# Odd attention of a two-layer decoder step: both units of a pair turned ahead of the next scores, a sample step's scores ahead of its key transposes

## The chip, the cores and the metric

The kernel runs on one core of a Trainium2 chip. The time is device microseconds (us) of one execution; lower is better. TensorE (PE) multiplies and transposes, VectorE (DVE), ScalarE (ACT) and GpSimd (POOL) work element by element, SyncE (SP) starts most DMAs. The engines run their own instruction streams in program order and meet at semaphores.

## The reference

Two layers of a hybrid decoder are run for a prompt (512 tokens, width 1024) and for 8 samples of one token each with a cache of 256 positions. Layer 0 mixes with a gated convolution and a matrix memory, layer 1 with two attentions; an MLP with squared relu follows each. The change is in layer 1, in this part:

```python
def odd_attend(...):                       # per block of 128 queries; f32
    ...
    # compressed: softmax over 64-token blocks, o_c
    # selected (8 blocks at most, "s"), sliding window of 256 ("w"), and top-k keys of the indexer ("d"):
    s_w = jnp.einsum('btgrd,blgd->btgrl', qn, kw[:, :, 0]).astype(f32) * scale - m_n[:, :, None] * dist_w[...]
    p_w = masked_softmax(s_w, mask_w[:, None, None, :])
    o_w = jnp.einsum('btgrl,blgd->btgrd', p_w.astype(kw.dtype), kw[:, :, 1])
    o_n = gates[..., 0:1] * o_c + gates[..., 1:2] * o_s + gates[..., 2:3] * o_w
    ...
    o_d = jnp.einsum('btgrk,btkgd->btgrd', p_d.astype(sel_d.dtype), sel_d[:, :, :, 1]).reshape(bn, tq, -1)
```

The samples' attention is the same over their cached keys and one new key. Every branch has 8 heads in 2 groups.

## The kernel before, in words

All weights stream through a ring in SBUF; the projections and the MLPs are long runs of matmuls 128x128 by 260 (line 1024), with each operand split into a high and a low part. Between the odd layer's input projection and its output projection lies the attention stage.

The prompt's attention is cut into 96 **units**: one block of 128 queries (i), one head (p of 4, g of 2) and one branch ("d", "s" or "w"). A unit has 1 to 4 key blocks of 128. Units u and u+1 with u even are a **pair**: the same queries, branch and p, for g = 0 and 1. The first 32 units are of branch d, the next 32 of s and w for query blocks 2 and 0, the last 32 of s and w for blocks 1 and 3. For one unit the work goes round the engines:

- `pair_scores` (line 1488): PE forms the scores of both units of a pair, in banks 0 and 1. It waits for `q_sc`, VectorE's reduction of the pair before.
- line 2694: VectorE adds the position table and finds the row's extreme, then counts `q_sc`.
- line 1909: ScalarE forms the exponential and its sum (ACTIVATE and a read of the accumulator), then counts `q_e`.
- `unit_turned` (line 1503): PE transposes the unit's 1 to 4 blocks into bank 2 (u even) or 3 (u odd). It waits for `q_e` of the unit and for `q_te`, u-1, which says that unit u-2 has been copied out of that bank.
- line 1920 (traced as line 1599, the helper): ScalarE copies the turned unit to SBUF and counts `q_te`.
- `pair_values` (line 1518): PE multiplies with the values, into bank 5 or 6; it waits for `q_te` of both units.
- `end_of` (line 1533): after the last unit of a job (one query block and branch), PE spreads the inverse sums, or adds the compressed branch, in bank 2.

The order is written out by a loop over steps t = 0 to 99 on each engine. In PE's loop (line 1561) step t has `unit_turned(t - 3)`; an odd step has also `pair_scores(t + 1)` and `pair_values(t - 5)`, and ends fall in odd steps. VectorE in step t reduces unit t. ScalarE in step t (line 1902) forms the exponential of unit t, then copies unit t - 3, then does sample work; from step 70 it also converts a weight tile in every third step. So ScalarE copies unit t - 4 right after the exponential of unit t - 1.

Sample work is laid between the units: in PE's even steps t = 12 + 2k runs `sample_step(k)` (line 1378), in the odd ones after them `sample_rest(k)`. Four times, from k = 0, 10, 19 and 28 on, `cached_keys(st, ...)` (line 1353) runs for st = 0 to 4: it transposes cached keys of two samples into bank 4 (st 0 to 3) and forms the scores of the two samples turned in the step before (st 1 to 4). ScalarE copies the turned keys into one of two buffers, `kTs`, and counts `bt_ev`. Both parts of `cached_keys` wait for the same value of it. Transposes are traced as line 982, all other matmuls of the stage as line 986; a transpose is 128x128, scores use 64 rows (64*128), values 64 columns (128*64), sample matmuls 32 or 64 columns.

Of the kernel before, what the change touches and what calls it, by code (L numbers as in the profile page):

```python
# [49 lines left out]
LS = PAST + 1  # L50
# [27 lines left out]
def build(nc, x_prompt, x_sample, state_conv, state_C, state_n, state_m, cache_kv, cache_idx, cache_win, page_table,  # L78
# [20 lines left out]
    with ExitStack() as ctx:  # L99
# [3 lines left out]
        def sem(name):  # L103
            return ctx.enter_context(nc.semaphore(name))
# [30 lines left out]
        ps = [ctx.enter_context(nc.psum_tensor(f"ps{i}", [P, 512], F32)) for i in range(8)]  # L135
# [21 lines left out]
        sm = {n: sem(n) for n in names}  # L157
# [378 lines left out]
        kTs = [room[:, 2 * LS * i:2 * LS * (i + 1)].rearrange("p (b k) -> p b k", b=2) for i in range(2)]  # L536
# [70 lines left out]
        units = []  # L607
# [371 lines left out]
        def _(pe):  # L979
            def tr(out, in_, n):  # L980

                return pe.matmul(out, in_, ident[0:n, 0:n], start=True, stop=True, is_transpose=True,  # L982
                                 skip_group_check=True)

            def mm(out, lhsT, rhs, start=True, stop=True):
                return pe.matmul(out, lhsT, rhs, start=start, stop=stop, skip_group_check=True)  # L986
# [166 lines left out]
            for k in range(KD):  # L1153
                last = tr(ps[7][:, B * k:B * k + B], xs_stage[:, P * k:P * k + P], B)
# [35 lines left out]
            for idx in range(len(E_TILE)):  # L1190
                if idx:
                    split_tile(G_IN0 + idx, xh1, hl)
                if idx == 5:
                    pe.wait_ge(sm["wc_in"], 16 * 8)
                    for s in range(2):
                        last = tr(ps[7][:, BLK * s:BLK * (s + 1)], wcK[0:64, P * s:P * s + P], 64)
                    last.then_inc(sm["tin"], 1)
                if idx == 2:
# [4 lines left out]
                    for half in range(2):  # L1203
                        last = mm(ps[4 + half][0:4, 0:H2], ident[0:8, 4:8], gz[:, half * H2:(half + 1) * H2])
                    last.then_inc(sm["fg_mm"], 1)
                if idx == 12:
# [7 lines left out]
                    for i in range(4):  # L1214
                        last = tr(ps[7][:, 16 * i:16 * i + 16], scs[:, P * i:P * i + P], 2 * B)
# [4 lines left out]
                if idx in (16, 18, 20, 22):  # L1220
# [6 lines left out]
                    for n, t0 in ((4, 12), (6, 16)):  # L1227
                        for b in range(B):
                            last = tr(ps[n + b // 4][:, P * (b % 4):P * (b % 4) + P],
                                      big[:, t0 + h, S + b:S + b + 1].to_broadcast([P, P]), P)  # L1230
                    last.then_inc(sm["head_mm"], 1)
                if idx == 25:
# [3 lines left out]
                    for i in range(4):  # L1236
                        last = tr(ps[5][0:B + 2, P * i:P * i + P], big[:, i, S - 2:T], P)
# [9 lines left out]
            for h in range(MH):  # L1247
# [6 lines left out]
                for n, t0 in ((2, 20), (3, 16)):  # L1254
                    for i in range(QT):
                        last = tr(ps[n][:, P * i:P * i + P], big[:, t0 + h, P * i:P * i + P], P)
# [3 lines left out]
                for i in range(QT + 1):  # L1260
# [5 lines left out]
                    if i >= 1:  # L1266
                        j = i - 1
                        pe.wait_ge(sm["p_ok"], QT * h + j + 1)
                        if j == 0:
# [8 lines left out]
                           stop=(j == QT - 1)).then_inc(sm["pv_mm"], 1)  # L1278
# [3 lines left out]
                for j in range(QT):  # L1282
                    last = mm(ps[4][:, 0:P], vw[:, P * j:P * j + P], ktm[:, P * j:P * j + P], start=(j == 0),
                              stop=(j == QT - 1))
                last.then_inc(sm["cn_mm"], 1)
                for j in range(QT):
                    last = mm(ps[5][0:1, 0:P], wsc[:, j:j + 1], ktm[:, P * j:P * j + P], start=(j == 0),
                              stop=(j == QT - 1))
# [21 lines left out]
            for idx, name in enumerate(O_NAMES):  # L1310
# [6 lines left out]
                if 4 <= idx <= 6:  # L1317
# [7 lines left out]
                    for c0 in range(0, i + 1, 2):  # L1325
                        c1 = min(c0 + 2, i + 1)
                        for e in range(4):
                            if n and not c0:
                                pe.wait_ge(sm["isc_r"], 4 * (n - 1) + e + 1)
                            r = slice(32 * e, 32 * e + 32)  # L1330
                            last = mm(ps[4 + e][:, P * c0:P * c1], big[r, L["qi"], P * i:P * i + P], kiz[r, P * c0:P * c1])
# [14 lines left out]
            for s, name in enumerate(SLOTS):  # L1346
                if s >= 4:
                    pe.wait_ge(sm["tm_a"], s - 3)
                for i in range(QT):
                    last = tr(ps[4 + s % 4][:, P * i:P * i + P], big[:, L[name], P * i:P * i + P], P)  # L1350
                last.then_inc(sm["tm_mm"], 1)

            def cached_keys(st, n0, lhs_of, src_of, key_rows, acc_rows):


                if 0 <= st < 4:
                    if n0 + st:
                        pe.wait_ge(sm["bt_ev"], n0 + st)
                    else:
                        pe.wait_ge(sm["pct_ev"], 1)  # L1360
                    for b in range(2):
                        for t in range(2):
                            last = tr(ps[4][0:key_rows, 256 * b + P * t:256 * b + P * t + P], src_of(2 * (st + 4 * b) + t), P)
                    last.then_inc(sm["bt_mm"], 1)
                if 1 <= st <= 4:
                    pe.wait_ge(sm["bt_ev"], n0 + st)
                    for b in range(2):
                        bb = st - 1 + 4 * b
                        r = 32 * b if acc_rows == 64 else 0
                        last = mm(ps[7][r:r + 32, 0:LS], lhs_of(bb)[:, r:r + 32], kTs[(st - 1) % 2][0:key_rows, b, :],  # L1370
                                  start=(st == 1 and r == 32 * b), stop=(st == 4 and (b == 1 or acc_rows == 64)))
                    last.then_inc(sm["bs_mm"], 1)

            def new_col(j, col):

# [91 lines left out]
            def compressed_step(t):  # L1467

                if 1 <= t <= QT:
                    pe.wait_ge(sm["kc_ok"], 1)  # L1470
                    i = t - 1
                    for p in range(NP):
                        last = mm(ps[7][:, 64 * i + 16 * p:64 * i + 16 * p + 16], big[:, L[f"qn{p}"], P * i:P * i + P], KCZ)
                    last.then_inc(sm["pc_mm"], 1)
                if t == QT:
                    for p in range(NP):
                        last = tr(ps[4][0:64, P * p:P * p + P], VF[:, p, :], P)
                    last.then_inc(sm["vf_mm"], 1)
                if t == 10:
                    pe.wait_ge(sm["vf_ev"], 1)  # L1480
                    pe.wait_ge(sm["pc_n"], 1)
                    for i in range(QT):
                        last = tr(ps[4][0:64, P * i:P * i + P], sc[:, 64 * i:64 * i + 64], P)
                    last.then_inc(sm["pct_mm"], 1)
# [3 lines left out]
            def pair_scores(u):  # L1488

                i, p, _, br, k0, o = units[u]  # L1490
                q = L[f"q{'d' if br == 'd' else 'n'}{p}"]
                ends_at = sorted({min(i + 1, k0 + 2), i + 1})
                for c0, c1 in zip([k0] + ends_at, ends_at):
                    for g in range(2):
                        if u >= 2 and c0 == k0:
                            pe.wait_ge(sm["q_sc"], u + g - 1)
                        r = slice(HD * g, HD * g + HD)
                        last = mm(ps[g][:, P * (c0 - k0):P * (c1 - k0)], big[r, q, P * i:P * i + P],
                                  big[r, L["k" + br], P * c0:P * c1])
                        if c1 == i + 1:  # L1500
                            last.then_inc(sm["q_mm"], 1)

            def unit_turned(u):
                i, p, g, br, k0, o = units[u]
                pe.wait_ge(sm["q_e"], u + 1)
                if u >= 2:
                    pe.wait_ge(sm["q_te"], u - 1)
                if u + 1 in ends:
                    kind, x = ends[u + 1]
                    if kind == "sums":  # L1510
                        pe.wait_ge(sm["q_r"], x + 1)
                    else:
                        pe.wait_ge(sm["q_g"], end_no[kind, x] + 1)
                for b in range(i + 1 - k0):
                    last = tr(ps[2 + u % 2][:, P * b:P * b + P], Pb[u % 6][:, P * b:P * b + P], P)
                last.then_inc(sm["q_t"], 1)

            def pair_values(u):

                i, p, _, br, k0, o = units[u]  # L1520
                if u == first_of[o] and o >= 2:
                    pe.wait_ge(sm["q_g"], end_no["sums", o - 2] + 1)
                pe.wait_ge(sm["q_te"], u + 2)
                for b in range(i + 1 - k0):
                    for g in range(2):
                        r = slice(HD * g, HD * g + HD)
                        v = tm[:, k0 + b, P * VS[br] + HD * g:P * VS[br] + HD * g + HD]
                        last = mm(acc(o)[r, P * p:P * p + P], v, PTb[(u + g) % 4][:, P * b:P * b + P],
                                  start=(p == 0 and b == 0), stop=(b == i - k0))
                        if b == i - k0:  # L1530
                            last.then_inc(sm["q_o"], 1)
# [24 lines left out]
            for s, name in enumerate(SLOTS):  # L1556
                last = tr(ps[2 + s // 4][0:B, P * (s % 4):P * (s % 4) + P], big[:, L[name], S:T], P)
# [3 lines left out]
            for t in range(len(units) + 4):  # L1561
                if t == 3:
                    pe.wait_ge(sm["tms_ev"], 2)
                if 0 <= t - 3 < len(units):
                    unit_turned(t - 3)
                if t % 2 and t + 1 < len(units):
                    pair_scores(t + 1)
                if t % 2 and t >= 5:
                    pair_values(t - 5)
                if t in ends:  # L1570
                    end_of(t)
                compressed_step(t)
                if t >= START:
                    if (t - START) % EVERY == 0:
                        sample_step((t - START) // EVERY)
                    if (t - START) % EVERY == 1:
                        sample_rest((t - START) // EVERY)
# [1161 lines left out]
```

## Time and profile before

| | us |
|---|---|
| median of 3 runs | 1422.44 (1422.29 to 1427.97) |
| profiled execution, first to last instruction | 1421.2 |
| PE busy | 1366.7 |
| VectorE busy | 745.3 |
| ScalarE busy | 504.6 |
| attention stage | 807 to 981 |

The profile gives the span of one execution, from its first to its last instruction; for what lies around the span it has no figure of its own. "Busy" counts the time in which an engine has an instruction under way; starts of PE's matmuls are exact and their ends are modelled, so the distance from start to start tells what one costs. "Idle before" is time in which the engine had nothing under way, with the instruction that ended it.

### The profile page before, as it was taken

The page shows a single profiled execution, that of the slowest core. Times are in us where ns is not written, and L with a number is a line of the kernel's source. Part 1 is how long each engine was busy: PE and PEld are TensorE (multiplying, and loading weights), DVE is VectorE, ACT ScalarE, POOL GpSimd, SP SyncE. Part 2 cuts the span into 40 slices and gives each one's busy share as a digit, 9 for nine tenths or more (in the row PEclk, how much of TensorE's full clock was granted, in tenths as well). Part 3 has the DMA queues.
Part 4 walks back from the last instruction along what each step waited for, and adds up shares of the span by engine and source line. Part 5 has one row for each costly group of instructions (what it writes and reads, how often), then busy time and mean ns, then how long its engine had stood idle before and what let it go on. Part 6 is the DMA issues. An engine that isn't in the chain of part 4 may idle for free. (4 is left out here: it accounts for less than half of the span.)

```text
span 1421.2 us, 27641 instructions
## 1 busy us (share of the span) xinstructions
PE 1366.7 (96%) x11359; PEld 1287.3 (91%) x11359; DVE 745.3 (52%) x1378; ACT 504.6 (36%) x1004; POOL 397.1 (28%) x470
## 2 busy tenths in 40 slices
PE   6999998999999999999899999999999999999996
PEld 5999975899999999999899966667999999999996
DVE  3424777667434343343879856454774343343435
ACT  3321224345314023032542366786553032140311
POOL 3014423365101010014744473023652010010102
PEclk9999999999999999999999999999999999999998
DMA  5343170030323131312323226204113313132301
GB/s 156 125 114 107 43 238 6 3 119 31 126 83 117 63 119 60 119 60 52 60 90 60 64 82 216 61 2 120 64 56 120 119 60 119 60 119 69 110 31 60
DMA packets 87196, 123.86 MB, mean 87 GB/s; under 512 B 24438, under 2 KB 42302, under 8 KB 87040
## 3 DMA queue, kind: packets, MB, share of 16 engines
q1 hardware_dynamic: 82048, 107.00, 23.6%
q0 software_dynamic: 5024, 15.10, 3.6%
q8 instruction: 91, 1.49, 0.4%
q14 instruction: 33, 0.27, 0.1%
HBM read 115.62 MB, written 8.57 MB: 87 GB/s over the span
## 5 line engine op out<-in xcount | busy, mean ns | idle before, releaser
L1024 PE MATMUL ps<-xh,ring_lo 128*128 128x260 f32 (+2 forms) x2496 | 503.5, 283 | 1.4 <-ACT big L1599 1.4
L1024 PEld LDWEIGHTS ps<-xh,ring_lo 128*128 128x128 f32 (+2 forms) x2496 | 382.6, 187 | 3.3 <-ACT big L1599 2.3
L1024 PE MATMUL ps<-xl,wr 128*128 128x260 f32 x1568 | 351.4, 283 | 6.1 <-DVE xl L2070 3.9
L1024 PE MATMUL ps<-xh,wr 128*128 128x260 f32 x1568 | 352.9, 284 | 2.5 <-POOL xl L824 1.2
L1024 PEld LDWEIGHTS ps<-xl,wr 128*128 128x128 f32 x1568 | 255.2, 188 | 8.2 <-DVE xl L2070 5.1
L1024 PEld LDWEIGHTS ps<-xh,wr 128*128 128x128 f32 x1568 | 256.0, 188 | 5.0 <-ACT att L1636 1.4
L842 POOL TENSOR_TENSOR att<-att 128x520 f32<-128x520 f32 (+1 forms) x80 | 77.3, 967 | 548.6 <-DVE att L1996 521.5
L1972 DVE TENSOR_TENSOR ring_lo<-ring,wr 128x1024 fp32r<-128x1024 f32 (+1 forms) x144 | 192.1, 1337 | 62.1 <-ACT wr L1599 62.0
L1024 PE MATMUL ps<-hh,wr 128*128 128x260 f32 x1024 | 222.1, 283 | 0.0
L1024 PE MATMUL ps<-hh,ring_lo 128*128 128x260 f32 x1024 | 221.8, 283 | 0.0
L1024 PE MATMUL ps<-hl,wr 128*128 128x260 f32 x1024 | 221.7, 283 | 0.0
L1599 ACT ACTIVATE wr<-ring 128x1024 fp32r<-128x1024 f32 (+1 forms) x162 | 167.4, 1049 | 130.1 <-PE ps L1024 120.4
L1024 PEld LDWEIGHTS ps<-hh,wr 128*128 128x128 f32 x1024 | 164.5, 188 | 0.2 <-issue 0.2
L1024 PEld LDWEIGHTS ps<-hh,ring_lo 128*128 128x128 f32 x1024 | 164.5, 188 | 0.0
L1024 PEld LDWEIGHTS ps<-hl,wr 128*128 128x128 f32 x1024 | 164.0, 188 | 0.0
L1636 ACT ACTIVATE att<-ps 128x260 f32<-128x260 f32 x64 | 24.6, 384 | 304.4 <-PE ps L1024 304.4
L1983 DVE TENSOR_TENSOR xT<-xT,ps 128x260 f32<-128x260 f32 x96 | 37.5, 422 | 162.9 <-PE ps L1024 162.9
L1996 DVE TENSOR_SCALAR att<-ps 128x260 f32<-128x260 f32 x64 | 27.4, 428 | 137.4 <-PE ps L1024 137.4
L1024 PE MATMUL ps<-hl,ring_lo 128*128 128x260 f32 (+1 forms) x464 | 93.4, 283 | 0.0
L1599 ACT ACTIVATE big<-ps 128x260 f32<-128x260 f32 (+6 forms) x104 | 40.3, 402 | 148.5 <-PE ps L1024 133.2
L789 POOL TENSOR_TENSOR ring_lo<-ring,wr 128x1024 fp32r<-128x1024 f32 x18 | 43.3, 2412 | 109.8 <-ACT wr L1599 109.8
L986 PE MATMUL ps<-big 128*64 128x128 f32 (+3 forms) x504 | 66.7, 348 | 4.8 <-DVE small L2694 3.3
(354 smaller groups left out, 1620.8 us busy)
## 6 DMA issues: line engine op xcount, KB each, us to landing
ring<-in_w_up SPq DMA_DIRECT2D x16, 2048.0 KB, 7.9
ring<-in_w_down SPq DMA_DIRECT2D x16, 2048.0 KB, 7.9
ring<-in_w_in_e SPq DMA_DIRECT2D x9, 1024.0 KB, 5.6
ring<-in_w_in_e SPq DMA_DIRECT2D x2, 2048.0 KB, 8.8
ring<-in_w_out_e SPq DMA_DIRECT2D x2, 2048.0 KB, 8.8
ring<-in_w_in_o SPq DMA_DIRECT2D x16, 256.0 KB, 5.0
ring<-in_cache_kv POOLq DMA_DIRECT2D x32, 128.0 KB, 2.4
ring<-in_w_out_o SPq DMA_DIRECT2D x8, 512.0 KB, 8.9
```

Source lines behind the costliest of these rows:

```text
L789: pool.tensor_tensor(w_l, w_raw(u), w_h.bitcast(F32), ALU.subtract).then_inc(sm["w_lo_p"], 1)
L842: pool.tensor_tensor(hid[j % 2][:, cc], rel[j % 2][:, cc], rel[j % 2][:, cc], ALU.mult).then_inc(sm["hid_sq"], 1)
L986: return pe.matmul(out, lhsT, rhs, start=start, stop=stop, skip_group_check=True)
L1024: last = pe.matmul(bank(g, half)[0:width(g), 0:H2], w[:, k, :], x[:, k, cols(half)], start=first, stop=final)
L1599: return act.activation(out, in_, ACT.Copy, scale=scale)
L1636: act.activation(rel[j % 2][:, 0:H2], psA(g)[:, 0:H2], ACT.Relu).then_inc(sm["free_a"], 1)
L1972: dve.tensor_tensor(w_l, w_raw(u), w_h.bitcast(F32), ALU.subtract).then_inc(sm["w_lo"], 1)
L1983: last = (dve.tensor_tensor(x, x, y, ALU.add) if scale is None else dve.scalar_tensor_tensor(x, x, scale, y, ALU.mult, ALU.add))
L1996: dve.tensor_scalar(rel[j % 2][:, H2:T], psB(g)[:, 0:H2], 0.0, None, ALU.max).then_inc(sm["free_b"], 1)
```

## The change

In PE's loop an odd step t now turns unit t - 3 and unit t - 2, one behind the other, ahead of `pair_scores(t + 1)`; an even step turns nothing. In `cached_keys` the scores of the samples turned in the step before are formed first, and the next key transposes come behind them. Waits, banks and counts stay as they were, and no other engine's stream is touched.

```diff
@@ -1353,6 +1353,14 @@ def cached_keys(st, n0, lhs_of, src_of, key_rows, acc_rows):
+                if 1 <= st <= 4:
+                    pe.wait_ge(sm["bt_ev"], n0 + st)
+                    for b in range(2):
+                        bb = st - 1 + 4 * b
+                        r = 32 * b if acc_rows == 64 else 0
+                        last = mm(ps[7][r:r + 32, 0:LS], lhs_of(bb)[:, r:r + 32], kTs[(st - 1) % 2][0:key_rows, b, :],
+                                  start=(st == 1 and r == 32 * b), stop=(st == 4 and (b == 1 or acc_rows == 64)))
+                    last.then_inc(sm["bs_mm"], 1)
                 if 0 <= st < 4:
                     if n0 + st:
                         pe.wait_ge(sm["bt_ev"], n0 + st)
@@ -1362,14 +1370,6 @@
                     last.then_inc(sm["bt_mm"], 1)
-                if 1 <= st <= 4:
-                    ...                                  (the eight lines above)
@@ -1561,8 +1561,9 @@
             for t in range(len(units) + 4):
                 if t == 3:
                     pe.wait_ge(sm["tms_ev"], 2)
-                if 0 <= t - 3 < len(units):
+                if t % 2 and 0 <= t - 3 < len(units):
                     unit_turned(t - 3)
+                    unit_turned(t - 2)
                 if t % 2 and t + 1 < len(units):
                     pair_scores(t + 1)
                 if t % 2 and t >= 5:
```

## Rows read from the trace of the kernel before

**Rows 1.** The page: span, and engines' busy time, share of span, instructions.
```profile
span 1421.2 us, 27641 instructions
PE 1366.7 (96%) x11359; PEld 1287.3 (91%) x11359; DVE 745.3 (52%) x1378; ACT 504.6 (36%) x1004; POOL 397.1 (28%) x470
```
**Rows 2.** Busy time by stretch: stretch, length, engines, granted PE clock, DMA, GB/s.
```profile
821.06:835.30 14.24, 11.90 (x79) 8.43 (x79) 8.26 (x29) 6.55 (x20) 10.41 (x17) 0.76 0.05 8
835.30:980.95 145.65, 139.41 (x1404) 96.18 (x1402) 79.05 (x297) 102.97 (x315) 40.88 (x53) 1.00 0.36 101
```
**Rows 3.** PE's waits in 807 to 981: total us, times, longest.
```profile
PE ps L986 <- DVE small L2694: 3.3, 4, 1.9
PE ps L986 <- ACT att L1599: 1.8, 5, 0.8
PE ps L986 <- ACT big L1599: 1.7, 3, 0.8
PE ps L986 <- DVE ring L2590: 0.7, 1, 0.7
```
**Rows 4.** Timeline of PE around 883: start, us, instruction, count, idle before.
```profile
882.30 0.33 PE L982 MATMUL ps<-ident,big 128*128 128x128 f32 x1
882.56 0.49 PE L986 MATMUL ps<-big 64*128 64x128 f32 x4
...
883.78 0.33 PE L982 MATMUL ps<-ident,big 128*128 128x128 f32 x1
883.95 0.60 PE L982 MATMUL ps<-ident,ring 128*128 128x128 f32 x4
884.48 0.63 PE L986 MATMUL ps<-ring,small 128*32 128x257 f32 x4
```
**Rows 5.** Timeline of all engines in step 45.
```profile
890.80 0.56 DVE L2694 CUSTOM_DVE_ANT_0 att<-small,ps 128x384 f32<-128x384 f32 x1 [1.58 <-PE ps L986]
...
891.40 0.61 ACT L1909 ACTIVATE att<-att,small 128x384 f32<-128x384 f32 x1 [0.25 <-DVE small L2694]
...
891.65 0.72 PE L986 MATMUL ps<-big 64*128 64x128 f32 x4
...
891.92 0.19 ACT L1909 ACTIVATION_READ_ACCUMULATOR att<-att,small 128x1 f32 x1
...
892.01 0.47 ACT L1599 ACTIVATE att<-ps 128x384 f32<-128x384 f32 x1
...
892.53 0.88 PE L986 MATMUL ps<-att,big 128*64 128x128 f32 x12 [0.15 <-ACT att L1599]
```
**Rows 6.** Timeline in steps 13, 29 and 93: exponential and scores.
```profile
835.98 0.72 ACT L1909 ACTIVATE att<-att,small 128x512 f32<-128x512 f32 x1 [1.64 <-DVE small L2694]
...
836.65 0.49 PE L986 MATMUL ps<-big 64*128 64x128 f32 x4
...
867.35 0.61 ACT L1909 ACTIVATE big<-big,small 128x384 f32<-128x384 f32 x1 [1.60 <-DVE small L2694]
...
867.37 1.17 PE L986 MATMUL ps<-big 64*128 64x256 f32 x4 [0.28 <-DVE small L2694]
...
969.54 0.61 ACT L1909 ACTIVATE att<-att,small 128x384 f32<-128x384 f32 x1
...
970.28 0.70 PE L986 MATMUL ps<-big 64*128 64x256 f32 x4
```
**Rows 7.** Timeline of ScalarE in step 81.
```profile
949.37 1.05 ACT L1599 ACTIVATE wr<-ring 128x1024 fp32r<-128x1024 f32 x1
...
950.32 0.50 ACT L1909 ACTIVATE att<-att,small 128x256 f32<-128x256 f32 x1
```
**Rows 8.** Timeline of PE in step 9.
```profile
828.42 0.80 PE L986 MATMUL ps<-big 64*128 64x128 f32 x2 [1.89 <-DVE small L2694]
```
**Rows 9.** Timeline of PE at the end of the stage.
```profile
975.00 1.09 PE L986 MATMUL ps<-ident,small 128*64 128x128 f32 x16 [0.84 <-ACT att L1599]
...
976.89 0.52 PE L982 MATMUL ps<-ident,big 128*128 128x128 f32 x3 [0.31 <-ACT big L1599]
...
979.27 0.88 PE L986 MATMUL ps<-big 128*64 128x128 f32 x12 [0.58 <-ACT big L1599]
```

More of the change, by code:

```diff
@@ L1364, in cached_keys @@
                     last.then_inc(sm["bt_mm"], 1)
-                if 1 <= st <= 4:
[L1366 to L1372, printed above, removed]
             def new_col(j, col):
```

## The prediction

> **What bounds the kernel now.** I read the page first: TensorE (PE) is busy for 96% of the span, no other engine above 52% [rows 1]. So a change counts by the PE time that it takes out and by the PE idle time that it makes or closes. Then the stretches: the diff touches PE's order in the odd attention only, from 807 to 981 us. Past 835.3 us PE is busy 139.4 of 145.7 us at a granted clock of 1.00. In the 14 us before, it is busy 11.9 and the clock averages 0.76 [rows 2]. Third, PE's waits there: 3.3 us on the score reduction of VectorE, 3.5 us on ScalarE's copies, 0.7 us on the sample index scores [rows 3]. PE does one thing after another there, nearly gap-free, and everything after the stage starts when it ends. So what PE loses here reaches the end of the kernel one to one; nothing behind it (PE-bound multiplications) gives it back.
>
> Last, the order in time of single units, on which the prediction rests. I write T(u), S(u), V(u) for the turning (transposes), scores and values of unit u; R, E, C for VectorE's reduction, ScalarE's exponential and ScalarE's copy of the turned unit. Before, odd step t runs T(t-3), S of units t+1 and t+2, V of t-5 and t-4; even step t+1 runs T(t-2) and the sample work. After, odd step t runs T(t-3), T(t-2), S, V, and the even step only sample work.
>
> **Part 1: fewer changes of matmul shape (a gain).** A transpose inside a block of transposes costs 0.11 us. One alone between matmuls of other shapes takes 0.26 us to the next start (882.30 to 882.56); the one at 883.78 is first of a block and takes 0.17, and the four after it take 0.53, so the last one takes 0.20 [rows 4]. A block therefore costs 0.06 at its first and 0.09 at its last transpose on top: 0.15 us per block. Before, an even step with sample matmuls in it reads V | T | sample matmuls | T | S: two blocks. After, V | sample matmuls | T T | S: one. For steps that turn sample keys as well this needs the second edit, which puts the score matmuls first so that the key transposes join the next block. From the code such steps are: k = 1 to 7 and 9, 11 to 14, 18, 20 to 23, 27, 29 to 32, 36, and step 4 with the compressed scores: 24, less the two (k = 20, 29) where sample transposes precede anyway. 22 x 0.15 = 3.3 us off. Steps without sample matmuls keep one block: nothing. Bounds: 0 to 24 x 0.15 = 3.6.
>
> Here the Trainium skill would argue otherwise. "TensorE: Matmul & The Clock Gate", Part 3, under what overlaps and what doesn't, says that a weight load overlaps matmuls in flight only when the row groups differ. Transposes use all rows, so by that a transpose next to a transpose would overlap as little as one next to a matmul, and merging blocks would save nothing. This trace doesn't agree: 0.11 us inside a block against 0.17 and 0.20 at its ends.
>
> **Part 2: the wait that the second transpose brings forward (a loss).** T(t-2) writes the bank that unit t-4 used, so it waits for C(t-4) (semaphore q_te). ScalarE works in program order: C(t-4) stands behind E(t-1), which needs R(t-1), which needs S(t-1), and S(t-1) was issued one odd step earlier. Before, the same C(t-4) was awaited by V in step t, behind S(t+1), and by T(t-2) after that. Now T(t-2) stands ahead of S(t+1), so the chain S, R, E, C, T, S closes once per pair of units. Behind the waiting transpose stand S, V, the end and sample work; R and E of the next pair wait for that S.
>
> Worked out for step 45 [rows 5]: R(44) starts 890.80, E(44) runs 891.40 to 892.11 with its accumulator read, C(41) 892.01 to 892.48, and V starts 892.53 after a wait of 0.15. T(43) can't start before 892.53 either. PE would be free for it at 891.65 (start of S(46)) less 0.09 (no change of shape there) less 0.33 (the three transposes of unit 41, done a step earlier): 891.24. Idle: 1.29 us. The chain from score end (890.77) to T is 1.76 us; PE has only V(38,39) and T(42) to fill it.
>
> The same subtraction for each odd step (end of the exponential, plus the copy's end 0.18, 0.28, 0.38 or 0.49 us behind it for 1, 2, 3 or 4 blocks, plus 0.05, less PE's free time) gives a positive wait in: step 13 1.21, 41 0.59, 45 1.29, 49 0.57, 61 1.29, 65 0.58, 75 0.44, 79 1.32, 91 0.62, 93 0.80. Sum 8.7 us. First and last: E(12) starts 835.98 and S(14) at 836.65; E(92) starts 969.54 and S(94) at 970.28 [rows 6]. In all other steps past 31 sample work, an end or both fill the 1.0 to 1.8 us of the chain. The pattern: a wait comes where the step has no sample matmuls, ahead of pairs whose chain is long (units of 2 to 4 blocks).
>
> Three places where another engine is late anyway:
> - Steps 27, 29, 31: VectorE is full with the sample's top-k; E(28) starts only at 867.35, S(30) at 867.37 [rows 6]. Waits of 0.4, 1.1 and 0.2 us appear, 1.7 together, but the S wait (0.28) and the index wait (0.68) [rows 3] fall inside them: 0.7 net.
> - Step 81: E(80) starts 950.32, behind a weight copy of 1.05 us on ScalarE [rows 7]. As it stands T(79) would wait 1.66; if S(80) comes late by step 79's wait, ScalarE has caught up and it is 0. I take 0.8.
> - Step 9: S(11) waits for VectorE until 828.42 in any case, 1.89 us [rows 8]. T(7)'s wait (1.2) falls into that, and T(7) itself (0.26) now fills idle time, as T(5) does ahead of S(9) (0.4, of a wait of 0.45; I take half): a gain of 0.5.
>
> After each wait the first transpose pays its 0.06 again: 13 x 0.06 = 0.8.
>
> Removed: V no longer waits for C(t-4), it came first: 0.15 + 0.16 + 0.42 + 0.19 = 0.9 (part of [rows 3]). At the end of the stage PE waits for the end's copy at 975.00 (0.84), at 976.89 (0.31) and for the last unit's copy at 979.27 (0.58) [rows 9]. T(93) now goes ahead of 975.00 and T(95) ahead of V(92), so the last V follows at once and the last end finishes about 0.8 earlier.
>
> **Part 3: sample steps.** kTs is copied by ScalarE after the key transposes and awaited by the next sample step's first instruction, as before, two steps later. The transposes end some 0.6 us later, the copy takes 0.6 + 0.2, and PE has T, T, S, V (2 us and more) in between. Hidden; if it weren't, PE would lose at most the 0.3 us that the transposes of a unit covered before, in each of 16 steps: 0 to 4.8, and I take 0. Key copies stand in ScalarE ahead of the next exponential, but that waits for S anyway. No DMA or GpSimd instruction is moved.
>
> **Sum.** +8.7 +0.7 +0.8 +0.8 -0.5 -0.9 -0.8 -3.3 = +5.5 us. Against the profiled span of 1421.2 that is 1426.7; the median of the runs (1422.44) is 1.2 above the span, and carried over this gives 1427.9. Ends of the unknown terms: Part 2 from 8.7 - 1.5 (chains counted 0.1 long in 13 steps) to 8.7 + 1.7 + 1.7 + 0.8; with the rest +3 to +9, that is 1425.4 to 1431.5 for this case alone.
>
> **Rivals.**
> - Other side: the loop doesn't bind, because ScalarE gets its copies out early once both units are turned early. For it: copies of second units waited for their late transposes. Against it: in step 45 ScalarE waited for VectorE, not for a transpose, ahead of E(44) [rows 5], and nothing in the change speeds S to R to E. Then Part 2 is 0 and -0.5 -0.9 -0.8 -3.3 = -5.5 remain: 1416.9. It decides if T(43) doesn't wait. With the clock's fall at 828 avoided as well (the second rival's price with the other sign, 3.4), 1413.5.
> - The clock falls once more. Granted clock went from 1.00 to half at 828 us, behind 1.9 us without a matmul [rows 8]; mean 0.76 over 14.24 us is 6.8 us at half clock, at most 3.4 us lost [rows 2]. New waits of 1.3 us come alone; the nearest kept clock is the 0.84 with 0.78, 0.31 and 0.58 around it [rows 9]. A fall in the cluster of steps 41 to 49: 1427.9 + 3.4 = 1431.3, two falls 1434.7.
> - Cancelling: chains shorter and step 81 free; within 2 us of before, say 1423.
> - Merged blocks save nothing, the shape change being paid by whatever stands there: +8.8, 1431.2. The page named above would say so; rows 4 speak against it.
>
> **How the numbers follow.** Chances: forecast 0.57, other side 0.13, clock 0.10, cancelling 0.15, no saving 0.05. Predicted 1427.9 us. Range 1419.0 to 1433.5: it leaves the other side's lower half and the second fall out. For this kernel 0.5% (7.1 us) is what can be told from no change. Slower by more: 0.20 of the forecast's 0.57, and the last and the clock rival: 0.35. Faster by more: the other side with the avoided fall: 0.06. Same: 0.59. Slower by anything at all: 0.8.
>
> **What would show it.** In the profile after: waits of a transpose on ScalarE's copy or on the unit's exponential of 0.5 to 1.3 us at some ten places, among them the pairs turned ahead of S(46), S(62) and S(80), and PE's waits on ScalarE rising from 3.5 us to 10 or more. V without a wait on a copy. One block of transposes where the sample matmuls stood between two; no start-to-start of 0.26 between sample matmuls and S. The stage from 807 us longer by 5 to 6 us and everything before and behind it equal. It is wrong if PE's idle time in the stage doesn't grow (other side), if blocks that are merged don't shorten their step by 0.15, or if the stage changes by another amount through a new stretch at half clock.

## The result, and the profile after

| | before | after |
|---|---|---|
| first comparison, median us (5 runs each) | 1422.59 | 1436.58 |
| profiled execution, span us | 1421.2 | 1428.5 |
| attention stage in it, first transpose to first output matmul | 173.90 | 181.44 |
| all later runs of before, and all runs of after, median us | 1428.68 (125 runs) | 1435.91 (29 runs) |

The first comparison gives a ratio of 1.0079 (95% interval 1.0050 to 1.0109): slower, by under 1% but clear of no change. The runs of both kernels don't spread evenly, they sit on levels. The mean granted clock of a run, the average share of the full 2.4 GHz that TensorE was given, tells which one:

| mean granted clock of the run | before, us (median) | after, us (median) | difference |
|---|---|---|---|
| 0.994 and more | 1422.87 (21 runs) | 1430.46 (9) | +7.6 |
| about 0.990 and 0.991 | 1428.59 (56) | 1436.40 (13) | +7.8 |
| 0.989 and less | 1431.88 (38) | 1439.84 (6) | +8.0 |

(Ten runs of before at 0.993, median 1424.6, and one of after at 0.992, 1434.1, lie between.) So the change costs about 7.6 to 8.0 us at like clock, 0.53%. The rows group neighbouring values: at exactly 0.994, 0.991 and 0.988 the differences are 7.5, 7.2 and 8.7 us, the last from 5 and 6 runs. Of the first five runs of before three have times of the first row, of the first five of after only one: of the 14 us between the first medians, about 6.4 were that draw.

The profiled executions are both of the first row (mean clock 0.994), each with one stretch of 6.8 us at half clock in the stage, and can be compared directly. First the page and the stage of the kernel after (columns as in [rows 1, 2]):

```profile
span 1428.5 us, 27641 instructions
PE 1363.6 (95%) x11359; PEld 1286.8 (90%) x11359; DVE 745.6 (52%) x1378; ACT 503.2 (35%) x1004; POOL 397.8 (28%) x470
```
```profile
806.79:988.23 181.44, 161.49 (x1590) 115.34 (x1588) 96.19 (x354) 117.98 (x360) 57.40 (x80) 0.98 0.30 83
```

PE is busy for less and the span is longer. In the stage before, PE was busy 164.56 of 173.90 us; now it is 161.49 of 181.44. So 3.1 us of work are saved and 10.6 us of idle time are made, +7.5. The work behind the stage starts 7.3 us later and takes as long as before: 435.2 and 435.3 us from its first matmul to the start of the last. PE's waits in 807 to 989 us, against [rows 3]:

```profile
PE ps L982 <- ACT att L1600: 9.2, 10, 1.2
PE ps L982 <- ACT big L1600: 4.2, 8, 1.2
PE ps L986 <- DVE small L2695: 1.6, 2, 0.9
PE ps L986 <- DVE small L2636: 1.3, 1, 1.3
PE ps L982 <- DVE ymix L2673: 0.8, 2, 0.5
PE ps L982 <- ACT ymix L1600: 0.7, 2, 0.5
PE ps L986 <- ACT att L1600: 0.7, 1, 0.7
PE ps L986 <- DVE small L2638: 0.6, 1, 0.6
PE ps L986 <- DVE small L2619: 0.5, 1, 0.5
```

The waits on ScalarE's copies are now those of the transposes (L982), 13.4 us in 18 places, where [rows 3] had 3.5 us, of values and ends (L986). One of them in order of time, all engines, from the scores of units 48 and 49 to the next scores (step 49):

```profile
896.33 1.29 PE L986 MATMUL ps<-big 64*128 64x256 f32 x12
897.28 0.56 DVE L2695 CUSTOM_DVE_ANT_0 att<-small,ps 128x384 f32<-128x384 f32 x1 [1.23 <-PE ps L986]
...
897.55 0.64 PE L986 MATMUL ps<-ring 128*32 128x128 f32 x16
...
897.88 0.62 ACT L1910 ACTIVATE att<-att,small 128x384 f32<-128x384 f32 x1 [1.28 <-DVE small L2695]
...
898.13 0.33 PE L982 MATMUL ps<-ident,big 128*128 128x128 f32 x1
...
898.50 0.47 ACT L1600 ACTIVATE att<-ps 128x384 f32<-128x384 f32 x1
...
899.11 0.30 PE L982 MATMUL ps<-ident,big 128*128 128x128 f32 x1 [0.66 <-ACT att L1600]
...
899.34 0.49 PE L986 MATMUL ps<-big 64*128 64x128 f32 x4
```

Here the chain S, R, E, C, T, S closes within one pair: VectorE had been idle for 1.23 us and ScalarE for 1.28 before the newest scores reached them, the copy of unit 45 follows the exponential of unit 48, and the transpose of unit 47 (899.11) starts 0.14 us after it ends. Unit 46's transpose (898.13) had no wait. The values of step 49 follow the scores with no wait of their own.

### The profile page after: what moved, and what is told of

Same layout as the page of the kernel before. It is cut to its first block and busy times, and to the rows that moved or that the text cites. A ratio compares the mean times of both kernels' runs of the same rounds, so it can differ in the third digit from the quotient of the medians.

```text
span 1428.5 us, 27641 instructions
## 1 busy us (share of the span) xinstructions
PE 1363.6 (95%) x11359; PEld 1286.8 (90%) x11359; DVE 745.6 (52%) x1378; ACT 503.2 (35%) x1004; POOL 397.8 (28%) x470
## 5 line engine op out<-in xcount | busy, mean ns | idle before, releaser
L1024 PEld LDWEIGHTS ps<-hl,ring_lo 128*128 128x128 f32 (+1 forms) x464 | 70.3, 185 | 0.6 <-DVE hl L2171 0.2
```

Of the source, the lines that this page charges most:

```text
L1024: last = pe.matmul(bank(g, half)[0:width(g), 0:H2], w[:, k, :], x[:, k, cols(half)], start=first, stop=final)
```

## The experiments

Each kernel's stage time comes from its profiled execution, its runs are given with their clock where that matters. "Idle" is the stage less PE's busy time in it. "A fall" is a stretch in which the granted clock was half. The stage has one of 6.8 us in the profiles of before, after, e3, e4, e5, e10 and e15; where another kernel's stage has more or less, that is said.

**e1 and e15: the changed kernel again.** The same code.

> The changed kernel once more, for the spread of its runs and each run's granted clock. Theory A (waits of the second transpose, plus further falls of the granted clock): a run with one fall (mean clock 0.994) spans about 1428.5 us; each further fall of 6.8 us at half clock adds at most 3.4, so spans of 1432, 1435 and 1438 with mean clocks 0.992, 0.990 and 0.988, and no run under 1428. Theory B (the clock has nothing to do with it, the spread is another engine's or the DMAs'): the spans vary without the clock, or the stage's waits on ScalarE vary from run to run.

> The changed kernel a third time, for the shares of the clock levels. So far before had 16 of 96 runs at a mean clock of 0.994 or more, and the changed kernel 6 of 17. Theory A (the levels are drawn alike, the change costs 7.5 us at each): again 7 to 8 us at equal clock, and at the medians of all runs; at least one run in six at 0.994 or more. Rival (the change adds falls): most runs at 0.991 or below and a difference of medians over 9 us.

Measured: medians 1435.93 (12 runs) against 1429.31, ratio 1.0046 (1.0025 to 1.0068), and 1435.84 (12 runs) against 1428.45, ratio 1.0056 (1.0034 to 1.0077). No run of the changed kernel is under 1429.9. The profile of e15 is one of mean clock 0.991, span 1435.0; its stage takes 181.38 us, the same as in the run of 1428.5. The windows of e15 show where the rest is, in layer 0 (columns as in [rows 2]):

```profile
195.00:209.60 14.60, 11.71 (x80) 9.56 (x79) 12.55 (x15) 5.83 (x14) 2.53 (x6) 1.00 0.70 256
209.60:216.50 6.90, 6.90 (x10) 2.87 (x9) 0.42 (x1) 0.00 (x0) 0.40 (x2) 0.51 0.68 253
216.50:254.00 37.50, 33.15 (x149) 19.40 (x147) 27.82 (x35) 15.47 (x37) 13.92 (x22) 1.00 0.02 6
254.00:257.50 3.50, 3.50 (x5) 1.51 (x5) 3.43 (x3) 0.00 (x0) 0.00 (x0) 0.51 0.00 0
```

There are two falls to half clock, 6.8 and 3.4 us long, in the matrix memory's heads, code that the change doesn't touch. The stage begins 6.6 us later (813.35 against 806.79), but not all of that is the two falls. Ahead of the first of them e15 is already 2.0 us behind; the first line is from the first profile of the changed kernel, the second from e15:

```profile
207.35 1.12 PE L986 MATMUL ps<-small 4*128 4x512 f32 x2 [2.18 <-POOL att L894]
```
```profile
209.31 1.75 PE L986 MATMUL ps<-small 4*128 4x512 f32 x2 [2.18 <-POOL att L894]
```

Most of those 2.0 us were lost near the start of the kernel: between 18 and 21 us PE was busy throughout in both, but started 29 matmuls in the first profile and 16 in e15. That leaves 4.6 us for the two falls, inside theory A's bound of half their length (5.1). The profiles of e3 to e8 and e14 show falls at the same two places, in PE's old order (e3, e5) and in the new. The changed kernel had 3 runs of 12 at a clock of 0.994, before 5 of 29 in the same comparison at 0.994 and more; over all runs it is 9 of 29 against 21 of 125. Nothing says that the change draws the slower levels more often, and with three profiles of the changed kernel whose stages agree in their waits, theory B of e1 has nothing for it.

**e2: only the loop's edit; e3: only the sample step's edit.**

```diff
# e2, against the kernel before (cached_keys stays as it was)
-                if 0 <= t - 3 < len(units):
+                if t % 2 and 0 <= t - 3 < len(units):
                     unit_turned(t - 3)
+                    unit_turned(t - 2)
# e3, against the kernel after (cached_keys stays changed)
-                if t % 2 and 0 <= t - 3 < len(units):
+                if 0 <= t - 3 < len(units):
                     unit_turned(t - 3)
-                    unit_turned(t - 2)
```

> Only the loop's edit: both units turned ahead of the scores, cached keys in the old order. Theory A: all waits of the changed kernel are there (about 14 us on ScalarE's copies), and the blocks of transposes are not merged in the 10 to 12 steps with both key transposes and sample scores, so it is 1.5 to 1.8 us slower than the changed kernel at the same number of clock falls: span about 1430 with one fall. Theory B (the reordered sample step makes the loss, by a late kTs copy): it would be near the kernel before, 1421 span.

> Only the sample step's edit: scores first, key transposes last, prompt units turned as before. Theory A: no new wait, the same number of blocks of transposes, so the time of before within 1 us (span 1421, one clock fall). Theory B (late kTs copy): 2 to 5 us slower, with waits of sample scores on ScalarE's ring copies.

Measured, e2: stage 184.14 us, PE idle in it 19.42, profiled span 1431.9, best run 1432.12 (clock 0.995). Nearly all the idle time of the changed kernel (19.95) is there without the sample step's edit. The best run, the only one at such a clock, is 1.7 us above the changed kernel's level there (1430.5), as theory A put it. Its profile has an extra fall in the cluster of waits behind step 45:

```profile
880.00:897.00 17.00, 15.11 (x150) 10.25 (x148) 6.91 (x31) 12.56 (x44) 0.00 (x0) 1.00 0.24 85
897.00:900.50 3.50, 3.50 (x19) 2.58 (x18) 0.80 (x3) 0.81 (x3) 0.00 (x0) 0.51 0.00 0
```

Behind 1.9 us of idle time, in pieces of 0.7 and 1.2, the clock was halved for 3.4 us. In the changed kernel's three profiles it stayed at 1.00 there.

Measured, e3: stage 173.35, idle 9.33, runs 1422.03 to 1431.24, ratio to before 0.9985 (0.9965 to 1.0004). There is no new wait, and the late kTs copy costs nothing. Theory B falls for both.

**e4: ScalarE copies first in even steps; e5: the same in the kernel before.**

```diff
+                if t % 2 and t < len(units):
+                    exponential(t)              # the lines that stood here, as a function
                 if ends.get(t - 1, ("", 0))[0] == "sums":
                     inverse_spread(ends[t - 1][1])
                 ...copy of unit t - 3...
+                if t % 2 == 0 and t < len(units):
+                    exponential(t)
```

> The changed kernel, and on ScalarE an even step copies the turned unit before it forms its exponential, so that the copy that the second transpose waits for no longer stands behind the exponential of the newest scores. Theory A: the waits of the second transpose go (14 us on ScalarE falls under 5), merged blocks keep their 3.3 us, so the span is 1415 to 1419, with one clock fall or none. Rival: the exponentials get late instead, and the first transposes wait for them: span 1424 or more. Theory B of the sample step: still 1428.

> Control: the kernel before with ScalarE's even step copying before its exponential. Theory A: in the old order only the values wait for the copy, 0.9 us in all, so it is worth at most that: attention stage 173 to 174 us (before 173.9). Rival (the swap is a gain of its own, 8 us, whatever PE's order): stage near 166.

Measured, e4: stage 173.26 us against 181.44, idle 11.58 against 19.95, PE busy 161.68 against 161.49. The same waits as above, in its stage:

```profile
PE ps L986 <- DVE small L2701: 2.6, 2, 1.9
PE ps L986 <- DVE small L2642: 1.3, 1, 1.3
PE ps L982 <- ACT big L1600: 1.2, 3, 0.8
PE ps L986 <- DVE ring L2597: 1.1, 1, 1.1
PE ps L986 <- ACT att L1600: 0.9, 1, 0.9
PE ps L982 <- DVE ymix L2679: 0.8, 2, 0.5
PE ps L982 <- ACT att L1600: 0.7, 1, 0.7
```

The transposes' waits on copies fall from 13.4 to 1.9 us, by nothing but the place of the copy in ScalarE's order. So the loss is the chain through the newest exponential. 8.2 us of stage come back. Against before, e4 has 2.9 us less work and 2.2 us more idle time: most of the merged blocks' gain is eaten by other waits. Best run 1422.98; ratio to before 1.0003 (0.9983 to 1.0022), a tie, where theory A had hoped for a span under 1419. e5: stage 176.18, idle 10.78. The swap alone is no gain in the old order. Its stage is 2.3 us longer, more than theory A allowed for (the wait on ScalarE's copy near the stage's end is 1.43 us, at 980.4, where before has 0.84), though the runs don't tell the two apart: ratio 1.0002 (0.9981 to 1.0023). The rival, a gain of its own, falls clearly.

**e6: the second unit turned late in twelve steps.**

```diff
+            LATE = (13, 29, 41, 45, 49, 61, 65, 75, 79, 81, 91, 93)
                 if t % 2 and 0 <= t - 3 < len(units):
                     unit_turned(t - 3)
-                    unit_turned(t - 2)
+                    if t not in LATE:
+                        unit_turned(t - 2)
+                if t - 1 in LATE:
+                    unit_turned(t - 3)
```

> The changed kernel, with the second unit turned late, as before, in the twelve odd steps 13, 29, 41, 45, 49, 61, 65, 75, 79, 81, 91 and 93 in which the working put a wait. Theory A: no waits on the copy there, merged blocks in the other steps: stage 171 to 172 us (changed kernel 181.4, before 173.9), PE idle in it about 9 to 10 us. Rival (the steps influence each other, waits move on to steps that had none): stage 174 to 178.

Measured: stage 177.42 us, idle 11.81, ratio to before 1.0020 (0.9993 to 1.0048). Most of the long waits are gone (idle 20.0 to 11.8) but the stage misses 171 to 172. Two things stand against it: waits remained in the steps next to them (0.37 and 0.21 on copies in steps 27 and 31, and the sample waits told of below), and the clock fell once more, for 3.4 us, where there are only short waits:

```profile
866.00:876.80 10.80, 9.53 (x90) 6.56 (x89) 9.81 (x41) 6.36 (x23) 4.88 (x9) 1.00 0.76 236
876.80:880.30 3.50, 3.50 (x25) 2.75 (x22) 1.98 (x10) 1.68 (x5) 1.54 (x3) 0.51 0.42 126
```

At equal clock (0.995) its best runs are 1423.75 and 1425.31 against 1422.9 of before: no gain. The rival was right that waits move on.

**e7: both units in one piece, but behind the scores.** The order in an odd step is S, T, T, V.

> Both units turned in one piece, but behind the next scores instead of ahead of them. Theory A (the loss is the place ahead of the scores, which closes the chain once per pair): no chain through the scores, the transposes wait for the copy only as the values did: stage 172 to 175 us, PE idle under 11. Rival (turning both units in one piece is itself the loss, since values and copies bunch up): stage 178 or more.

Measured: stage 181.13, but 17.1 us of it at half clock (13.7 of them at 823.5 to 837.2 us), against 6.8 in the kernels before and after; idle 12.47, of which 2.89 is the wait for VectorE near 840. Best runs 1426.61 and 1426.73 at clock 0.994, 3.8 us under the changed kernel at that level and as much over before. In PE's idle time theory A is nearly right (12.5 against 19.9), in the stage time it isn't: the profile is of a run with a longer half-clock part, so the stage can't be set against the others. The run is inconclusive on the size; if its two best runs are taken, the place ahead of the scores makes about half of the loss, which is an estimate and not shown.

**e8, e13, e14: VectorE's last part of the compressed scores one step later.** e8 is e6 with it, e13 the kernel before, e14 is e4.

```diff
             def compressed_step(t):          # VectorE
-                if t == 8:
+                if t == 9:
                     dve.wait_ge(sm["pc_e"], 1)
```

> e6 with VectorE's second part of the compressed scores moved from step 8 to step 9, behind the reduction that S(11) waits for; the wait of 1.9 us at 826 us goes. Theory A on the clock (idle time ahead of it makes it fall): the granted clock doesn't fall at 828 us, so the stage is 1.9 us of wait plus up to 3.4 us shorter than e6: 166 to 169 us. Rival (the fall has another cause): it falls there as before, stage 169 to 171.

> The kernel before, with VectorE's last part of the compressed scores moved from step 8 to step 9, behind the reduction that S(11) waits for. Theory A (the idle time of 1.9 us makes the fall at 828 us): the wait goes, and the fall with it in the runs at the best level; stage 173.9 - 1.9 - 3.3 = 169 us, best runs 1417 to 1418. Rival (the fall comes in any case, from the idle times of 0.7 and 0.45 before it): stage 172, best runs 1420.5.

> The same move in the changed kernel with ScalarE's copy first (e4, best run 1423.0, stage 173.3, where that wait was 1.9 us). Theory A: best runs 1417 to 1418, stage 168 to 169. Rival: stage 171 to 172, best runs 1421.

Measured, e13: stage 169.65 us against 173.90, span 1416.5; PE's timeline in step 9, against [rows 8]:

```profile
825.61 0.77 PE L986 MATMUL ps<-big 64*128 64x128 f32 x4
826.32 1.09 PE L986 MATMUL ps<-att,big 128*64 128x128 f32 x16
827.34 0.33 PE L982 MATMUL ps<-ident,att 128*128 128x128 f32 x1
828.08 0.60 PE L982 MATMUL ps<-ident,big 128*64 128x128 f32 x4 [0.41 <-DVE big L2548]
```
```profile
806.63:976.28 169.65, 161.98 (x1590) 114.16 (x1588) 96.30 (x354) 119.03 (x360) 57.35 (x80) 1.00 0.32 89
```

The four score matmuls follow each other without a break, where [rows 8] had 1.89 us of idle time between two and two, the granted clock of the whole stage is 1.00, and PE's busy time falls from 164.56 to 161.98 because nothing runs at half clock. Best run 1417.86 against 1421.39, median 1423.44 (11 runs) against 1428.45, ratio 0.9974 (0.9948 to 1.0000). Theory A on the fall holds here: idle time gone, fall gone. e14: stage 169.78, again none of it at half clock, but layer 0's two falls in the profiled run; best run 1422.24, median 1424.65, ratio 0.9989 (0.9966 to 1.0012). Its best runs miss the 1417 to 1418 of theory A: none is at a clock over 0.994. But e14 and e4 were profiled with the same two falls in layer 0, and there they ran 1424.83 and 1429.10 us, so the gain of the stage (3.5 us) reaches the end. e13 and e14 are also the one pair without half clock in the stage that differs by PE's order (and ScalarE's): PE's work is 161.98 and 159.38, so the merged blocks save 2.6 us there, and idle time is 7.67 and 10.40, so the waits take it back. e8: stage 174.87, which misses both its marks, best run 1422.12, falls of 3.4 us at 832 and at 873 us: there the early transpose of step 9 keeps a wait of 1.17 us at 830, and the clock still fell.

**e9, e10, e11: dummy matmuls in layer 0.** They stand in the first and the fourth memory head, in the kernel before, in the kernel after and in e4:

```diff
+                        if j == 0:
+                            ...the waits for vt_ok, den_ok and num_ok, from below...
+                            keep_busy(6, {0: 8, 3: 6}.get(h, 0))
                         pe.wait_ge(sm["p_ok"], QT * h + j + 1)
```

> The kernel before, with 8 and 6 dummy matmuls of 0.26 us in layer 0's first and fourth memory head, where the profiles of runs at mean clock 0.991 show a fall to half clock (at 208 and 252 us) behind PE idle times of 2.2 and 1.7 us. Theory A (which of the levels 1422, 1429 and 1432 us a run lands on is set by those falls, before and after alike): the levels at 1429 and 1432 go and the median is 1422 to 1424. Rival (the levels come from elsewhere): they stay, median 1428 to 1430.

> The changed kernel with the same dummy matmuls in layer 0. Theory A: median 1429.5 to 1431, that is 7 to 8 us over the padded kernel before, which is the change's own loss; the other 6 us between the first medians were falls of the clock in layer 0. Rival (the change itself makes more falls, in its own stage): median 1433 or more.

> The changed kernel with ScalarE's copy first in even steps and with the dummy matmuls. Theory A: 1421 to 1423, level with or a little under the padded kernel before (stage 173.3 against 173.9), and 6 us and more under the unpadded kernel before at its median. Rival: the attention stage falls to half clock once more in most runs, 1424 to 1427.

Measured: e9 median 1428.58 (12 runs), e10 1434.47 (10), e11 1429.35 (12). The levels stay, and all three medians miss theory A's (e11 also its rival's 1424 to 1427). The level at clock 0.994 moved from 1422.9 to 1425.9 (the dummies aren't free). The profile of e9 has no fall in the padded heads but four elsewhere, the longest of them 13.7 us at 819:

```profile
819.00:833.00 14.00, 14.00 (x73) 11.52 (x74) 4.74 (x16) 5.02 (x17) 5.35 (x10) 0.51 0.07 14
```

e11's profile has the same long one, at 817.5; e10's has only the 6.8 us in the stage that after has. In all three the falls in the padded heads are gone, and 14 of the 34 padded runs are at 0.994, where 6 of 33 of before are in the same comparison; but others take their place, so theory A falls as stated. In the 2 us ahead of e9's long fall stands a single idle time of PE, 0.74 us, which every profile has some 6 us into the stage. What e9 and e10 do show is the change's own cost once more: 1433.2 against 1425.9 at a clock of 0.994, +7.3, and 5.9 between the medians. e10's median is over the rival's 1433, but the dummies account for 3 us of it.

**e12: seven early turns in the kernel before.**

```diff
+            EARLY_T = (41, 45, 49, 61, 79, 91, 93)
-                if 0 <= t - 3 < len(units):
+                if 0 <= t - 3 < len(units) and t - 1 not in EARLY_T:
                     unit_turned(t - 3)
+                if t in EARLY_T:
+                    unit_turned(t - 2)
```

> The kernel before, with the second unit turned ahead of the scores only in steps 41, 45, 49, 61, 79, 91 and 93, which have no sample matmuls behind them: no block of transposes is saved. Theory A: the waits worked out for these seven add up, 6.5 us, less 0.7 that the values no longer wait: stage 179.5 to 180 us, PE idle 15 us. Rival (each step alone has slack, and only the whole sequence of early turns waits): stage under 176.

Measured: stage 176.59 us, 3.4 of it at half clock (before: 6.8), idle 13.37 against 9.34, ratio of the runs to before 1.0048 (1.0028 to 1.0067). PE at step 45:

```profile
892.92 0.27 PE L982 MATMUL ps<-ident,att 128*128 128x128 f32 x1
894.09 0.30 PE L982 MATMUL ps<-ident,att 128*128 128x128 f32 x1 [0.90 <-ACT att L1602]
```

0.90 us, where the changed kernel waits 1.23. The expectation had forgotten a term: with step 43 left in the old order, the three transposes of unit 41 (0.33) are still between the scores and this one and cover that much of the chain. With that term the wait is 1.29 - 0.33 = 0.96 for step 45. Together the seven waits are 4.2 us, where the changed kernel has 6.5 in the same steps. So both were partly right: single steps wait on their own, and turning the neighbours early as well takes 0.2 to 0.5 us of cover more from six of them. The seventh, step 93, whose neighbour 91 is early here too, waits 0.90 in both.

## Why the prediction was wrong, point by point

- **Part 1, merged blocks: right.** Forecast 22 blocks less and 3.3 us. The profiles have 74 blocks of transposes in the stage before and 51 after, 23 less, and PE's busy time is 3.07 us shorter, restarts included, 0.13 each; between e13 and e14, without half clock, it is 2.60 for as many, 0.11 each. With the loop's edit alone there are 61. By the Trainium skill ("TensorE: Matmul & The Clock Gate", Part 3, what overlaps and what doesn't) merging should have saved nothing, since a transpose uses all row groups and so shares them with any neighbour; the measurement decides against that reading.
- **Part 2, the waits: right in mechanism and place.** Forecast against measured in the ten steps: 13: 1.21, 1.19; 41: 0.59, 0.67; 45: 1.29, 1.23; 49: 0.57, 0.66; 61: 1.29, 1.23; 65: 0.58, 0.66; 75: 0.44, 0.38; 79: 1.32, 1.24; 91: 0.62, 0.54; 93: 0.80, 0.90. Sum 8.7 against 8.7. Step 81: 0.8 against 0.52. In steps 27, 29 and 31 the waits on copies are 0.37, 1.00 and 0.21, where 0.4, 1.1 and 0.2 were forecast. e4 shows the cause.
- **Part 2, the terms taken off: the mis-sized part.** "The last end finishes about 0.8 earlier" didn't happen: waits of 0.46, 0.69 and 0.79 us stand there in place of [rows 9]. And "in all other steps sample work, an end or both fill the chain" looked at one partner only. With its transposes gone from the even step, PE also reaches the sample matmuls and the ends sooner, and then waits for VectorE's or ScalarE's part of those:

```profile
937.22 0.63 PE L986 MATMUL ps<-ring,small 128*32 128x257 f32 x4 [0.57 <-DVE small L2638]
```
```profile
959.79 0.90 PE L982 MATMUL ps<-ident,att 128*128 128x128 f32 x4 [0.50 <-ACT ymix L1600]
```
```profile
972.28 0.63 PE L982 MATMUL ps<-ident,att 128*128 128x128 f32 x4 [0.50 <-DVE ymix L2673]
```

  With 0.53 at 860, 0.33 more at 906 and 0.30 at 968, and less the 0.29 that the last of the three had before, these make 2.4 us that no term held, and two of 0.21 on copies (930 and 964) make it 2.9. The end gave 1.0 less than forecast, step 9 0.2 less. On the other side two waits of before on the ends' copies (0.32 at 952.2, 0.78 at 973.5), which the sum had not counted either, went, and step 81 and steps 27 to 31 came out 0.4 smaller. Idle time grew by 10.6 us where the working had 8.0; busy time fell by 3.1 where it had 2.5 (3.3 saved, 0.8 for restarts). That is why +5.5 became +7.5 in the stage.
- **Part 3, the sample step: right.** e3 costs nothing and saves nothing that can be told.
- **Slips in the sums.** 13 steps at 0.1 are 1.3 and not 1.5 for the lower end. Both prices of the other side (1416.9 and 1413.5) lie under 1419.0, so the range left that rival out whole and not by half.
- **The clock.** "The clock falls once more" was priced at 3.4 a fall with a chance of 0.10, as something that the change would do, and the three runs shown were taken as the kernel's time. What the runs show is levels 6 and 9 us apart, before as after, and the profiles show where they come from: falls in layer 0 that come and go from run to run, and a start of the kernel that is up to 3 us slower (the matmul of 207.35 us above stands at 207.25 in e13 and at 210.28 in e12, ahead of any fall). The 1427.97 among the first three runs of before fits the second level (no clock is on record for it). Before's median over 125 runs is 1428.7. The change's own loss, 7.6 to 8.0 us, put on the median shown would be 1430.0 to 1430.4, inside the range; the five runs that were compared lay 6 us higher by the draw. So the step that failed is the one that carried a median of three runs over, "the median of the runs (1422.44) is 1.2 above the span", as if the kernel had one level: it put the step between levels at nothing, where the runs showed 5.9 us between the changed kernel's first two. The 2.0 us missing from the sum for the stage are the smaller part. A draw the other way would have put the same sum inside the range; that would have been luck.
- **The other side.** Theory "the loop doesn't bind" is refuted by every profile of the changed kernel.

What stays open: what decides in a run whether layer 0's falls come. They aren't tied to the change. Also open is why none of e14's 11 runs reached a clock over 0.994, where 4 of e13's did. The best version found is e13, the old order with VectorE's part moved: 0.26% faster than before by the ratio, with an interval that ends at 1.0000, so at the edge of what these runs can tell, and 3.5 us better at the best run; it owes nothing to the change.

## What to carry to other kernels

When a buffer-reuse wait is moved ahead of the instruction that feeds the same ring of engines, count how many turns of the loop the ring has. Here one order let copy and transpose run a pair behind the scores. The other closed score, reduction, exponential, copy and transpose in one pair, 1.8 us against 0.5 us of cover in step 45. Look at what stands before the awaited instruction on its own engine; swapping copy and exponential there took 8.2 us of stage back, what the change of order on TensorE had cost and a little more, but no more than a tie with the old order came of it. And ask for the levels of a kernel's runs before a gain of half a per cent is forecast from a median of three: with the mean clock of each run, runs of one level can be compared.

## What the runs showed of the hardware

- Where transposes stand between matmuls of other tile shapes, the start behind the last transpose came 0.09 us later than inside the block, and the start behind the first 0.06 later ([rows 4]: 0.20 and 0.17 against 0.11). 23 fewer blocks of transposes gave 3.07 us, and 2.60 without half clock.
- The granted clock fell from 2.4 to 1.2 GHz for 3.4, 6.8 or 13.7 us. In the stage it did so behind an idle time of 1.9 us in a piece (before, e3, e4, e5 and e12), behind 1.17 and 0.86 (after), 1.17 alone (e8), 0.67 and 1.22 (e2), and 0.37, 0.68 and 0.21 (e6). In e13 it did not, behind 0.68, 0.45 and 0.41 us, nor in e14 behind 0.71 and 0.68. But in e7, e9 and e11 it fell for 13.7 us about 2 us behind a single 0.75. So the length of the idle times alone doesn't tell whether the clock falls.
- A fall of 6.8 us in this stage cost less than 3.4 us: e13 has none and 2.6 us less work than before, and e1's profile has one of 3.4 us in place of 6.8 and its stage is 1.4 us shorter (180.02 against 181.44), with the same waits.
- One program has levels of time 6 and 9 us apart, which the mean granted clock (0.994, 0.991, 0.987 to 0.988) names run by run, if not wholly: TensorE's slower start in e15 (2.0 us by 207 us) stands in a stretch in which the profile shows a clock of 1.00.
